# Turning gathered expert rows: from TensorE and ScalarE to VectorE, with rows gathered in quarters

## The reference, cut to what matters

```
h = (_rms(x) * norm2_g[l] * (1.0 + sc2) + sh2)
scores = sigmoid(h @ router_w); idx = the 8 chosen experts of each token; wts = their weights
for each expert e, for the tokens t in its list:
    hid = silu(h[t] @ w1[e]) * (h[t] @ w3[e])        # w1, w3: 1024 x 256
    y[t] += (hid @ w2[e]) * wts[t, e]                # w2: 256 x 1024
y += (silu(h @ ws1) * (h @ ws3)) @ ws2
out = x + g2 * y
```

## Time and profile before

| | |
|---|---|
| median of 3 runs | 2582.93 us (2582.93 to 2586.4) |
| span of the profiled execution | 2584.8 us |
| its own time | not given apart from the three runs; the span lies among them |
| PE busy | 2512.4 us, 97% |
| PE weight loads (beside PE) | 1271.5 us, 49% |
| DVE / ACT / POOL busy | 1029.0 / 579.2 / 417.5 us |
| DMA moved | 440.86 MB, mean 171 GB/s |

### The profile page before, as it was taken

One profiled execution on the slowest core, in us unless ns is written; L12 is line 12 of the kernel. 1 busy time (PEld: TensorE's weight loads), 2 busy tenths in 40 slices (PEclk: granted clock), 3 DMA queues, 4 the chain that ended last, 5 costly groups with the idle time before them and its releaser, 6 DMA issues.

```text
span 2584.8 us, 35212 instructions
## 1 busy us (share of the span) xinstructions
PE 2512.4 (97%) x9350; PEld 1271.5 (49%) x9351; DVE 1029.0 (40%) x2548; ACT 579.2 (22%) x1078; POOL 417.5 (16%) x418
## 2 busy tenths in 40 slices
PE   6999999999999999999999999999999999999996
PEld 3444555555455556555444554445444444444443
DVE  3365443444465545554245756121222122222221
ACT  3311333332311331331111121111111111211110
POOL 0000000000210000000111435122222222222221
PEclk9999999999999999999999999999999999999998
DMA  9122243432723232222333116787889889989994
GB/s 269 52 49 75 77 116 96 107 109 73 200 54 82 82 94 80 76 96 95 124 108 133 58 41 235 260 263 230 256 277 360 289 284 344 349 269 330 344 295 92
DMA packets 128164, 440.86 MB, mean 171 GB/s; under 512 B 18220, under 2 KB 20404, under 8 KB 110928
## 3 DMA queue, kind: packets, MB, share of 16 engines
q1 hardware_dynamic: 86560, 306.91, 34.3%
q0 software_dynamic: 41520, 132.86, 19.7%
HBM read 369.85 MB, written 77.20 MB: 173 GB/s over the span
## 4 chain that ended last, share of the span: by engine, by line
PE 93%; DMA 4%; issue 1%; DVE 0%; ACT 0%; POOLq 0%; SPq 0%; POOL 0%; DVEq 0%
PE psum L862 34%; PE psum L1285 16%; PE psum L1342 8%; PE psum L1120 6%; PE psum L1137 4%; PE psum L1289 3%; PE psum L1253 3%; PE psum L1181 2%; PE psum L1077 2%; PE psum L1348 2%; DMA out_x<-mem,put 2%; PE psum L956 2%; PE psum L946 2%; PE psum L965 1%; DMA mem<-in_exp_w 1%; PE psum L1204 1%
## 5 line engine op out<-in xcount | busy, mean ns | idle before, releaser
L862 PE MATMUL psum<-mem 128*128 128x512 f32 x2048 | 910.1, 594 | 2.0 <-ACT mem L1485 2.0
L862 PEld LDWEIGHTS psum<-mem 128*128 128x128 f32 x2048 | 377.4, 191 | 416.9 <-issue 415.9
L1285 PE MATMUL psum<-mem 128*128 x1008 | 445.2, 597 | 6.6 <-issue 5.5
L1285 PEld LDWEIGHTS psum<-mem 128*128 128x128 f32 x1008 | 191.3, 191 | 253.9 <-issue 253.7
L1342 PE MATMUL psum<-mem 128*128 128x512 f32 x504 | 234.8, 598 | 2.0 <-DMA mem<-in_exp_w 1.0
L2402 DVE TENSOR_TENSOR mem<-mem,psum 128x256 f32<-128x256 f32 x93 | 39.2, 421 | 433.4 <-ACT mem L1736 428.1
L716 POOL DMA_INDIRECT out_x<-mem,put x93 | 142.6, 1534 | 345.8 <-issue 233.2
L1532 ACT ACTIVATE mem<-psum 128x512 f32<-128x512 f32 x128 | 75.8, 595 | 494.7 <-PE psum L862 491.9
L1736 ACT ACTIVATE mem<-psum 128x256 f32<-128x256 f32 x93 | 35.7, 384 | 615.6 <-PE psum L1285 491.6
L1120 PE MATMUL psum<-mem 128*128 128x512 f32 x384 | 165.0, 592 | 0.0
L712 POOL DMA_INDIRECT mem<-h_d,idx x93 | 95.4, 1026 | 390.0 <-DVE idx L2425 144.1
(11 more groups left out here) (378 smaller groups left out, 2370.4 us busy)
## 6 DMA issues: line engine op xcount, KB each, us to landing
mem<-in_exp_w SPq DMA_DIRECT2D x201, 1024.0 KB
mem<-in_w_in SPq DMA_DIRECT2D x16, 2048.0 KB, 13.9
proj_d<-mem SPq DMA_DIRECT2D x104, 256.0 KB, 2.0
mem<-in_ada_w POOLq DMA_DIRECT2D x16, 1024.0 KB, 6.0
mem<-proj_d POOLq DMA_DIRECT2D x56, 256.0 KB, 2.9
mem<-proj_d POOLq DMA_DIRECT2D x20, 512.0 KB, 4.8
mem<-in_ada_w SPq DMA_DIRECT2D x4, 2048.0 KB, 19.8
mem<-in_w_branch SPq DMA_DIRECT2D x3, 2048.0 KB, 8.0
```

What stands on the lines that cost most here:

```text
L862: mm = t.matmul(bank(unit_bank(u)), l, r, start=(k == 0), stop=(k == KD - 1))
L1285: return t.matmul(bank(4 + j), xgT[:, k, P * j:P * (j + 1)], up_piece(h, r, k), start=(k == 0), stop=(k == KD - 1))
```

## The change

Turning the gathered rows moves from PE and ACT to DVE. DVE's transpose works in blocks of 32 x 32. For that, a token row is gathered in four quarters of 256 features: lane 32i + b of `xg` gets, for each group of 32 tokens, quarter i of the token b. One DMA gathers 128 such quarters (one group of 32 tokens), so a tile takes four gathers and a half tile two. DVE then reads every eighth element (`g a k` as `g k a`), and the block transposes give lane p the feature 8p + k, as before.

What goes with it:

- `h2` and `h2_d` are in feature order. L2205 reads in a row; router and shared weights load as (k p), in runs of 256 bytes and 1 KB; one copy on ACT and its order for two modulation rows go.
- The row numbers are 4 x token + quarter, computed on DVE by a multiply and an add from `first4` (first three items, four small DMAs ahead of the large one) and `lists4` (all lists in the new layout, four DMAs, 2 MB in all, behind the gathers of items 0 and 1).
- `xgT` exists twice. PE's transposes, ACT's copies and the semaphores between them go; `e_T` takes their place, raised by DVE once per item, awaited by PE before the ups and by POOL before it reuses `xg`.
- The hidden rows' turns go to PSUM bank 1 instead of 5.

```diff
-        xgT = view(14336, KD, 2 * P)
+        xgT = [view(14336, KD, 2 * P), view(25600, KD, 2 * P)]
-            pool.wait_ge(s_mcc, 3)
+            pool.wait_ge(s_mcc, 2)
...
+            by_group = list_d.rearrange("(g b r) c -> b g r c", g=4, b=32)
+            for i in range(4):
+                g.dma_start(first4[32 * i:32 * i + 32], by_group[:, :, 0:3 * NT, :]).then_inc(s_l4, 16)
...
-            def gather(x, i, n):
-                return g.indirect_dma_start(x[0:n], None, h2_d, bass.IndirectOffsetOnAxis(ap=i[0:n], axis=0),
-                                            bounds_check=T - 1, oob_is_err=False)
+            h2_q = h2_d.rearrange("t (i f) -> (t i) f", i=4)
+            def gather(x, j, q, groups, s):
+                for n in range(groups):
+                    g.indirect_dma_start(x[:, 2 * P * n:2 * P * (n + 1)], None, h2_q,
+                                         bass.IndirectOffsetOnAxis(ap=idx[:, q, j, n:n + 1], axis=0),
+                                         bounds_check=4 * T - 1, oob_is_err=False).then_inc(s, 16)
...
             fetch_second(tokens(pool, 1), 1, 1)
-            pool.wait_ge(e_Tb[0], 1)
+            for i in range(4):
+                g.dma_start(lists4[32 * i:32 * i + 32], by_group).then_inc(s_l4, 16)
+            pool.wait_ge(e_T, 1)
...
-            def turn_rows(j, x):
-                for k in range(KD):
-                    mm = t.transpose(psum[:, 2 * j + k // 4, (k % 4) * P:(k % 4 + 1) * P], x[:, k * P:(k + 1) * P], ident[:, :])
...
-                    pe.wait_ge(e_xTa[0], now)
+                    pe.wait_ge(e_T, before)
...
-            def rows_turned(j, half):
-                s.activation(xgT[:, 4 * half:4 * half + 4, P * j:P * (j + 1)], bank(2 * j + half).rearrange("p (k n) -> p k n", n=P),
-                             ACT.Copy).then_inc((e_xTa, e_xTb)[half][j], 1)
...
-                link(v.scalar_tensor_tensor(out=z3, in0=turned(y), scalar=stat[:, 32 + i:33 + i], in1=a3, op0=ALU.mult, op1=ALU.mult))
+                link(v.scalar_tensor_tensor(out=z, in0=y, scalar=stat[:, 32 + i:33 + i], in1=a2b, op0=ALU.mult, op1=ALU.mult))
...
+            def turn_group(j, p, groups):
+                for _ in range(groups // 2):
+                    got[j][p].up()
+                got[j][p].wait(e_xg[j][p])
+                return v.transpose(xgT[p][:, :, P * j:P * j + 32 * groups].rearrange("p k (g b) -> p g k b", g=groups),
+                                   xg[j][p][:, 0:2 * P * groups].rearrange("p (g a k) -> p g k a", g=groups, k=KD))
...
+            turn_rows(tokens(dve, 0), 0)
             shared_out(7)
+            dve.wait_ge(s_ls, 16 + 16 * NT * TOPK + 16)
             put_lists()
...
+            dve.wait_ge(s_l4, 128)
...
                         n = tokens(dve, i)
+                        with dve.If(tokens(dve, i + 1) > 0):
+                            turn_rows(tokens(dve, i + 1), (q + 1) % 2)
```

More of the change, by code:

```diff
@@ L201, in layer_kernel @@
         lists = view(16384, NE * NT, 2)
-        lists2 = view(4096, NE * NT, 2)
+        lists2 = view(24576, NE * NT, 2)
+        lists4 = view(0, 4, NE * NT, 2)
         xg = [[view(12288, D), view(13312, D)], [view(20480, D), view(9248, D)]]
-        xgT = view(14336, KD, 2 * P)
+        xgT = [view(14336, KD, 2 * P), view(25600, KD, 2 * P)]
         ob = [[view(18432, D), view(19456, D)], [view(7168, D), view(21504, D)]]
@@ L758, in fetch_ahead @@
                 with pool.If(n_3 > 0):
[L759 removed]
+                    pool.wait_ge(e_T, now)
                     pool.wait_ge(e_idx, now)
@@ L1314, in up_first, with up_second @@
                     with pe.If(h > 0):
-                        up_half_first(2 + r, now)
+                        up_half_first(2 + r)
                     with pe.Else():
-                        up_half_first(r, now)
+                        up_half_first(r)
                     pe.nop()
                 pe.nop()
-            def up_second(n, h, r, before):
-                turned.wait(e_xTb[1])
-                pe.wait_ge(e_hc[0], before)
-                seconds.wait(e_hc[1])
-                pe.sem_inc(e_go, 1)
+            def up_second(n, h, r):
                 seconds.up()
@@ L1743, in _ @@
             act.wait_ge(e_clear, 1)
-            for x in (*e_xTa, *e_xTb, *e_si, *e_hc):
+            for x in (*e_si, *e_hc):
                 act.sem_inc(x, 1)
-            second, wide = Count(act, "second"), Count(act, "wide")
-            def copy_second():
-                second.up()
-                second.wait(e_Ta[1])
-                rows_turned(1, 0)
-                second.wait(e_Tb[1])
-                rows_turned(1, 1)
-            def copy_first(now):
-                act.wait_ge(e_Ta[0], now)
-                rows_turned(0, 0)
-                act.wait_ge(e_Tb[0], now)
-                rows_turned(0, 1)
-            with act.If(tokens(act, 0) > P):
-                copy_second()
-            act.nop()
-            copy_first(1)
+            wide = Count(act, "wide")
             def act_item(it, q):
                 i = 4 * it + q
-                n, n_next = tokens(act, i), tokens(act, i + 1)
+                n = tokens(act, i)
                 now = act.snap(i + 2)
@@ L1775, in act_item @@
                     silu(1)
-                act.nop()
-                with act.If(n_next > P):
-                    copy_second()
-                act.nop()
-                with act.If(n_next > 0):
-                    copy_first(now)
                 act.nop()
@@ L2370, in _, with turn_rows @@
             shared_out(6)
+            dve.wait_ge(e_clear, 1)
+            got = [[Count(dve, f"got{j}{p}", 0, 32) for p in range(2)] for j in range(2)]
+            def turn_group(j, p, groups):
[4 more added lines that the diff above has]
+                                   xg[j][p][:, 0:2 * P * groups].rearrange("p (g a k) -> p g k a", g=groups, k=KD))
+            def turn_rows(n, p):
+                with dve.If(n > HALF):
+                    with dve.If(n > P):
+                        with dve.If(n > P + HALF):
+                            turn_group(1, p, 4)
+                        with dve.Else():
+                            turn_group(1, p, 2)
+                        dve.nop()
+                    dve.nop()
+                    turn_group(0, p, 4).then_inc(e_T, 1)
+                with dve.Else():
+                    turn_group(0, p, 2).then_inc(e_T, 1)
+                dve.nop()
+            turn_rows(tokens(dve, 0), 0)
             shared_out(7)
+            dve.wait_ge(s_ls, 16 + 16 * NT * TOPK + 16)
             put_lists()
@@ L2424, in take_tokens @@
                 e = first_list(dve, 4 * it + q + 3)
-                v.tensor_copy(idx[:, (q + 3) % 4, :], some(lists, e, 2, 0)).then_inc(e_idx, 1)
+                v.tensor_scalar(idx[:, (q + 3) % 4, :, :], quarters(lists4[:, :, bass.ds(e, 2), 0:1]), 4.0, quad[:, :],
+                                ALU.mult, ALU.add).then_inc(e_idx, 1)
             def weigh(n, q, done, copied):
```

101 lines of the change are left out of this document (36 added, 65 removed).

## The result

The changed kernel takes 2571.3 us (median of 5 runs, 2570.0 to 2573.0) against 2582.93 us (2579.5 to 2586.4): a ratio of 0.9954, 95% interval 0.9942 to 0.9966. Faster by 12 us; I had forecast 39. The profiled spans are 2568.3 and 2584.8 us, 16.5 apart.

What follows compares the result with a forecast made beforehand. The prediction took TensorE as the bound, with DMA close behind in the expert stage. In us, -81 turns, +1 cover, -1 norm rows, +2 scatters, +25 DMA, +1.5 first up, +9 lists, +5 clock gave -38.5: 2544 us, range 2525 to 2562.

Steps and rivals of the forecast that it cites:

- turns leave TensorE: Expert stage: 93 tiles lose a block of 8 PE turns, 0.87 us each, so 81 us leave PE.
- runs under the up of item i ... costs PE nothing: DVE's turn of item i+1, 2.1 us per tile, hides under item i's up if rows arrive in time.
- +1 bare cover: Behind half tiles the half down barely covers SiLU, product and hidden turn: 0 to 3 us, taken as 1.
- +25 DMA: Expert stage: PE waits 25 us more as the DMA share rises to 0.96, bounds 5 and 60.
- It fits: POOL's 312 quarter gathers and 93 scatters total 592 us of about 900 us.
- 2 us on PE: Scatters queued behind later gathers leave 4 to 8 us later; DVE's longer wait costs PE 2 us.
- +9 lists: Stage start: DVE enters its loop only once lists4 land, at 1623; second up 9 us later, bounds 3 and 15.
- the 1.5 us put on the first up: Stage start: four gathers and DVE's turn put the first up at about 1610.5 against 1608.94.
- +5 clock: Two more places where the granted clock falls to 0.50 after waits, 2.8 us each, taken as 5 us.
- 2508 (nothing in the way): Rival for the expert stage: the DMA is not in the way, total 2508 us; chance 12%.
- 2572 (the DMA takes nearly all): Rival: DMA share can't rise above about 0.90, so the stage shrinks by only 16 us, total 2572; chance 13%.

Runs made afterwards that it cites:

- a6_eighth_turn: The changed kernel with VectorE turning only one eighth of each tile, the rest left as it was: 2549.5 us, ratio 0.9862.
- a3_half_weights: The changed kernel loading only half of w1 and w3 of each expert: 2606.4 us, ratio 1.0084 to the kernel before.
- b1_two_turns: The kernel before with 2 of the 8 TensorE turns of each item's first tile left out: 2568.2 us, ratio 0.9933.
- a1_again: The changed kernel with VectorE's wait for lists4 moved from ahead of the loop to its first use: 2597.6 us, ratio 1.0064.

## Why the prediction was wrong

The forecast of each step against the two traces, in us:

| step | forecast | measured |
|---|---|---|
| turns leave TensorE | -81 | -79 (91 tiles in the middle) |
| start, up to the second up | +9.5 | +16.4 |
| TensorE's waits in the middle | +28 (25 for weights, 2 scatters, 1 cover) | +31.7 (product +25.2, no named cause +10.6, weights -2.5, gathers -3.0, rest +1.4) |
| clock | +5 | +13.6 |
| tail | 0 | +0.7 |
| sum | -38.5 | -16.6 (spans: -16.5) |

- *"runs under the up of item i ... costs PE nothing"* is the step that failed. I put the turn at the start of the up. But DVE's round is a chain of its own: the weighing waits for the last down, and branches of over 2 us and the turn follow before the product. Behind a half up there is no room. The prediction had this place at *"+1 bare cover"*; TensorE's waits for the product are 25.2 us. The row of durations was right (2.01 us); the start was not read, though the weighing's row of before shows that DVE waits for the downs (161.3 us). a6_eighth_turn shows it: the turn shortened, 22 us come back.
- The number is off by 22 us, and by the table the middle's waits, being near their forecast by luck, are only 4 of them. The other 18 are the clock (9), the start (7) and the turns (2).
- *"+25 DMA"*: the size of the waits came out, with another cause, so by luck. TensorE waits 2.1 us for weights, and at the upper level halving w1 and w3 wins nothing (a3_half_weights): that speaks against the term for this kernel. b1_two_turns shows 9 us of it in the kernel before. Whether full DMA engines make the gathers land later, for which VectorE waits 26 us in the stage, no run separates. Two numbers that agree don't make a mechanism.
- *"It fits", "2 us on PE"* for GpSimd: its queue wasn't full, but the order in it (scatter, then four issues per tile, then 6 us to land) lengthens the loop. Whole rows give 9.5 and 9.9 us, and in the kernel before four gathers per tile cost 35.
- *"+9 lists"*: the mechanism was right, the size was not. I took 7 us at 300 GB/s for 2 MB, issued by 1616; they were issued by 1609.4, but took 19.7 us, in a stretch (1607 to 1629) at a share of 0.96 and 261 GB/s, shared with weights and gathers. a1_again gives 12.8 us for it at the upper level. (The sooner lists and the 1.5 us put on the first up went the other way: it began 1.4 us sooner than before.)
- *"+5 clock"*: the same instructions take 13.6 us longer. That more and scattered gaps are the reason is argued from the granted clock, 0.99 before and 0.96 after in the stage, and not tested.
- The rivals: 2508 (nothing in the way) and 2572 (the DMA takes nearly all). The second has nearly the measured time, 2571, for the wrong reason: the DMA share didn't rise.

## What to carry to other kernels

Work moved to an idle engine costs nothing only if that engine is free at the time when it is wanted: look up what releases each piece of its round and where the shortest tile leaves it, not its busy share. Splitting a gather in four is paid in the issuing queue's order, even where the bytes and the queue's share of time stay. Measure the unaltered kernel beside every variant, and on more than one chip: a change can have a level that the kernel before doesn't have.

## What the runs showed of the hardware

- A 32 by 32 transpose of 1024 fp32 per lane on VectorE takes 1228 ns reading in a row and 2010 ns with a step of 32 bytes; 512 with the step 1103 ns. The Trainium skill (SBUF — State Buffer, "Door 1: The DMA port swizzle", the note on cachelines) says that fp32 reads stride freely up to four elements, 16 bytes, and that each access that crosses to a new line pays. The trace agrees that a step of 32 bytes pays; no run here gives this operation a step between 4 and 32 bytes.
- A gather takes GpSimd 1015 ns on average (before 1026). The 58 that overlap a turn on VectorE by more than 0.2 us take 1001 ns, the 252 others in the stage 1017: no hold-up of their issuing by this operation.
- ScalarE up to 8 us late just behind rows of indirect DMA issues, on three of five chips, seen only in kernels with quarter gathers and VectorE's turns.
